# Four small edits in the opening of a two-layer transformer trunk: constant transfers later and in larger pieces, norm weights turned on chip, the shift row turned ahead of the scale row, identity products in TensorE's first wait

## What is computed

```python
for i in range(2):
    mod = silu(c) @ ada_w[i] + ada_b[i]                       # ada_w[i]: 1024 x 6144
    sh_a, sc_a, g_a, sh_f, sc_f, g_f = split(mod, 6)
    h = rmsnorm(x, norm_mix[i]) * (1 + sc_a) + sh_a
    y = diff_attention(h, ...) if i == 0 else retention(h, ..., ret_gn)
    x = x + g_a * y
    h = rmsnorm(x, norm_ffn[i]) * (1 + sc_f) + sh_f
    x = x + g_f * moe(h, router_w[i], ...)                    # 64 experts, 8 per token, one shared
return rmsnorm(x, final_norm)
```

## Time and profile before

| | us |
|---|---|
| median of 3 executions | 1393.24 (1391.47 to 1395.55) |
| the profiled execution | 1395.63 |
| its span in the trace | 1393.7 |
| PE busy in it | 1316.4 |
| DVE, ACT, POOL busy in it | 546.0, 458.4, 227.3 |

### The profile page before, as it was taken

How to read it: one execution, slowest core, us unless ns; L and a number is a source line. 1 busy time by engine, 2 the same in 40 slices (tenths; PEclk the granted TensorE clock), 3 DMA queues, 4 the chain that set the end, 5 groups by cost and what they waited for, 6 DMA issues and landing times.

```text
span 1393.7 us, 32787 instructions
## 1 busy us (share of the span) xinstructions
PE 1316.4 (94%) x11645; PEld 853.6 (61%) x11646; DVE 546.0 (39%) x1259; ACT 458.4 (33%) x938; POOL 227.3 (16%) x684
## 2 busy tenths in 40 slices
PE   4899899999999999899899999999999999999986
PEld 2888675556465555554598778765555565555543
DVE  2565684323232322222634355753323233223324
ACT  3444552222222222212544464622222222222212
POOL 8200103111111211111100000021111111112110
PEclk8899999999999999999999999999999999999998
DMA  9988989999999999999996344599999999999994
GB/s 358 340 316 316 406 363 406 420 421 422 422 422 422 422 422 422 422 422 420 381 377 205 135 151 151 220 402 380 423 422 421 422 421 422 422 423 421 421 422 202
DMA packets 105783, 516.02 MB, mean 370 GB/s; under 512 B 10280, under 2 KB 30880, under 8 KB 55808
## 3 DMA queue, kind: packets, MB, share of 16 engines
q1 hardware_dynamic: 101728, 509.64, 90.8%
q0 software_dynamic: 3296, 3.50, 0.9%
q10 hardware_dynamic: 704, 2.10, 0.4%
HBM read 514.11 MB, written 1.09 MB: 370 GB/s over the span
## 4 chain that ended last, share of the span: by engine, by line
PE 67%; SPq 16%; DMA 9%; DVE 4%; ACT 2%; issue 2%; ACTq 0%; DVEq 0%
PE bank L1007 17%; PE bank L1219 14%; SPq L365 7%; PE bank L1186 7%; PE bank L1145 7%; PE bank L1222 7%; PE bank L1247 6%; SPq L368 4%; DMA ring<-in_exp_w_dram 4%; PE bank L1253 3%; SPq L359 3%; PE bank L981 2%; DMA mods<-in_exp_w_dram 2%; DMA ring<-in_da_w_in_dram 2%; DMA ring<-in_sh_w_dram 1%
## 5 line engine op out<-in xcount | busy, mean ns | idle before, releaser
L1219 PE MATMUL bank<-ring,arena 128*64 128x512 f32 x768 | 184.6, 616 | 15.8 <-DMA ring<-in_exp_w_dram 15.8
L1186 PEld LDWEIGHTS bank<-arena 128*128 128x128 bf16 x3264 | 142.1, 98 | 55.5 <-issue 55.5
L1145 PE MATMUL bank<-arena_r 128*128 128x512 f32 x560 | 159.9, 422 | 3.0 <-DVE arena_r L1683 3.0
L1676 DVE SCALAR_TENSOR_TENSOR arena<-bank,arena 128x128 f32<-128x128 f32 x103 | 32.9, 348 | 327.2 <-ACT arena L762 327.2
L1683 DVE TENSOR_TENSOR arena_r<-bank,arena_r 128x512 fp32r<-128x512 f32 x136 | 94.1, 692 | 154.1 <-ACT arena_r L769 154.1
L1186 PE MATMUL bank<-arena 128*128 128x64 bf16 (+1 forms) x3264 | 151.8, 207 | 0.0
L762 ACT ACTIVATE arena<-bank 128x256 f32<-128x256 f32 (+1 forms) x68 | 22.6, 333 | 387.0 <-PE bank L1219 279.1
L579 POOL TENSOR_TENSOR arena<-arena,pass_base 128x2 f32 x136 | 26.4, 218 | 735.2 <-PE bank L1194 569.0
L769 ACT CAST arena_r<-bank 128x512 fp32r<-128x512 f32 x136 | 79.8, 587 | 175.1 <-PE bank L1247 112.3
L1219 PEld LDWEIGHTS bank<-ring,arena 128*64 128x64 f32 x768 | 66.6, 141 | 113.2 <-issue 107.6
L1663 DVE TENSOR_SCALAR arena<-bank,mod_T 128x128 f32<-128x128 f32 x272 | 92.9, 405 | 70.0 <-PE bank L1186 70.0
(11 more groups left out here) (277 smaller groups left out, 2130.3 us busy)
## 6 DMA issues: line engine op xcount, KB each, us to landing
ring<-in_exp_w_dram SPq DMA_DIRECT2D x264, 1024.0 KB, 24.1
ring<-in_ada_w_dram SPq DMA_DIRECT2D x48, 1024.0 KB, 12.3
mods<-in_exp_w_dram SPq DMA_DIRECT2D x40, 1024.0 KB, 25.0
HH<-in_exp_w_dram SPq DMA_DIRECT2D x40, 1024.0 KB, 21.1
arena<-in_exp_w_dram SPq DMA_DIRECT2D x40, 1024.0 KB, 26.0
ring<-in_ret_w_in_dram SPq DMA_DIRECT2D x24, 1024.0 KB, 12.8
ring<-in_da_w_in_dram SPq DMA_DIRECT2D x12, 1024.0 KB, 14.8
ring<-in_ret_w_out_dram SPq DMA_DIRECT2D x8, 1024.0 KB, 4.9
```

The source lines that it names most:

```text
L1145: ins = nc.tensor.matmul(banks[4 + NH * tc + hf][:, :], S[:, P * tc:P * tc + P], y[:, r, 512 * hf:512 * hf + 512], start=False, stop=(last ...
L1186: ins = nc.tensor.matmul(banks[2 - 2 * half][:, P * kk:P * kk + 2 * W], parts[:, tc, r, P * (4 * half + kk):P * (4 * half + kk + 1)], Pg[: ...
L1219: ins = nc.tensor.matmul(banks[1][W * i:W * i + W, :], xg[:, k, W * i:W * i + W], w13[j][:, k, :, :], start=(k == 0), stop=(k == KD - 1))
```

## The change

1. **Where the constants are transferred.** POOL waits for the end of the first projection (`proj_done` 1) before it starts the vectors for `lam` and the bias rows. `rw`, `rb` and `gn` come behind `store_rows(0, 2, 3, 3)`, which waits for three finished rows. The use of `lvec` on DVE and ACT (`lsum`, `lexp`, `nlam`) moves behind the split of tile 11 and the score masks.
2. **In what pieces.** `rw` is laid out by layer, so a partition's piece is 2 KB. `gn` comes as 16 rows of 512 bytes into the unused `ret_s` and is turned by one PE transpose in layer 1, with a copy on DVE.
3. **Shift row ahead of the scale row.** `turn_h` waits for the identity alone (`ident_ready`). The shift row is turned while the tiles of the scale row land; banks differ. DVE copies block pairs 0 and 1 of `hT`, ACT 2 and 3 (before: DVE 1, ACT 0, 2 and 3).
4. **Identity products.** 52 products of 128x128 (bf16, result unused) behind the turned scale row, ahead of the first projection.

```diff
-        rw = sb("rw", [P, KD, DEPTH * E])
+        rw = sb("rw", [P, DEPTH, KD, E])
+        rw_by_chunk = rw[:, :, :, :].rearrange("p l k e -> p k l e")
...
+        gn_rows = ret_s[0:16, 0:P]
...
+            pool.sem_inc(ident_ready, 1)
...
+            pool.wait_ge(decay_exp, RET_HEADS)
+            for hd in range(RET_HEADS):
+                ins = nc.gpsimd.affine_select(out=decay[:, hd, :], in_=decay[:, hd, :], compare_op=ALU.is_ge, fill=0.0,
+                                              base=0, pattern=[[1, T]], channel_multiplier=-1)
+            ins.then_inc(decay_ready, 1)
+            pool.wait_ge(proj_done, 1)
             for i, v in enumerate((da_lq1, da_lk1, da_lq2, da_lk2)):
                 pool.dma_start(lvec[:, i, :], v.broadcast_to([P, DA_DH])).then_inc(consts_in, 16)
             pool.dma_start(subg[:, :], da_subln.rearrange("a p -> p a"), allow_slow_non_contiguous=True).then_inc(consts_in, 16)
...
-                                              base=0, pattern=[[1, T]], channel_multiplier=-1)
-            ins.then_inc(decay_ready, 1)
+            for q in range(4):
+                pool.dma_start(browB[32 * q:32 * q + 1, :, :],
+                               ada_b[1:2].rearrange("a (s q n) -> q a s n", s=6, q=4)[q]).then_inc(rowsB_in, 16)
+                for i, g in enumerate((norm_mix, norm_ffn)):
+                    pool.dma_start(nrowB[32 * q:32 * q + 1, i, :], g[1:2, 256 * q:256 * (q + 1)]).then_inc(rowsB_in, 16)
+            store_rows(0, 2, 3, 3)
             for l in range(DEPTH):
-                pool.dma_start(rw[:, :, E * l:E * (l + 1)], router_w[l].rearrange("(p k) e -> p k e", k=KD)).then_inc(late_consts_in, 16)
+                pool.dma_start(rw[:, l, :, :], router_w[l].rearrange("(p k) e -> p k e", k=KD)).then_inc(late_consts_in, 16)
                 pool.dma_start(rb[:, l, :], router_b[l:l + 1, :].broadcast_to([P, E])).then_inc(late_consts_in, 16)
-            pool.dma_start(gn[:, :], ret_gn.rearrange("a (c p) -> p (a c)", p=P), allow_slow_non_contiguous=True
-                           ).then_inc(late_consts_in, 16)
-            store_rows(0, 2, 3, 3)
+            pool.dma_start(gn_rows, ret_gn.rearrange("a (c p) -> (a c) p", p=P)).then_inc(late_consts_in, 16)
             store_rows(1, 0, 2, 5)
             store_rows(1, 3, 2, 7)
             pool.wait_ge(rows_stored, 192)
...
-                by_act, by_dve = ((0, 2, 3), (1,)) if n == 0 else ((0, 2), (1, 3))
+                by_act, by_dve = ((2, 3), (0, 1)) if n == 0 else ((0, 2), (1, 3))
 
                 def evict(m):
...
+                        act.wait_ge(hT_dve, 2 * n + by_dve.index(m) + 1)
                     nc.scalar.copy(hT_hi[:, 2 * m:2 * m + 2, :], hT_full[:, 2 * m:2 * m + 2, :]).then_inc(hT_rounded, 1)
 
                 act.wait_ge(mod_T_in[n], 1 if n == 0 else 16)
-                evict(0)
+                evict(by_act[0])
                 round_high(0)
-                evict(2)
...
                 if n == 0:
-                    evict(3)
+                    round_high(1)
+                evict(by_act[1])
+                if n > 0:
+                    round_high(1)
                 round_high(2)
                 round_high(3)
...
-                nc.scalar.copy(rw_hi, rw[:, :, :]).then_inc(rw_rounded, 1)
+                nc.scalar.copy(rw_hi.rearrange("p k (l e) -> p k l e", l=DEPTH), rw_by_chunk).then_inc(rw_rounded, 1)
...
             round_w("mix_in", 0, 1)
-            act.wait_ge(lam_sums, 1)
...
+            nc.scalar.activation(lexp[:, :], lsum[:, :], ACT.Exp).then_inc(lam_exp, 1)
             exps(0)
...
+            act.wait_ge(gn_ready, 1)
...
-            ada(0, 0, banks[4][:, 0:256])
-            pe.wait_ge(pool_consts, 1)
+            ada(0, 0, banks[6][:, 0:256])
+            pe.wait_ge(ident_ready, 1)
             turn_h()
-            ada(0, 1, banks[4][:, 256:512])
-
-            pe.wait_ge(row0_ready, 2)
-            for s in range(2):
+
+            def turn_row0(s):
+                pe.wait_ge(row0_ready, s + 1)
                 for k in range(KD):
                     for q in range(4):
-                        ins = nc.tensor.matmul(banks[5][32 * q:32 * q + 32, KD * s + k:KD * s + k + 1],
+                        ins = nc.tensor.matmul(banks[5 + 2 * s][32 * q:32 * q + 32, k:k + 1],
                                                mrow0[:, s, k:256:KD], ident[:, 32 * q:32 * q + 1], start=True, stop=True)
-            ins.then_inc(rows0_turned, 1)
+                ins.then_inc(rows0_turned, 1)
+
+            turn_row0(0)
+            ada(0, 1, banks[4][:, 0:256])
+            pe.wait_ge(pool_consts, 1)
+            turn_row0(1)
+            for _ in range(52):
+                nc.tensor.matmul(banks[6][:, 0:P], ident16[:, :], ident16[:, :], start=True, stop=True)
 
...
+            pe.wait_ge(late_consts_in, 16 * 5)
+            nc.tensor.transpose(banks[7][:, 0:16], gn_rows, ident[0:16, 0:16]).then_inc(gn_turned, 1)
...
+                    evict(0)
                 evict(1)
                 if n == 0:
...
+            nc.vector.tensor_tensor(mrow0[:, 0, :], banks[6][:, 0:256], brow0[:, 0, :], ALU.add).then_inc(row0_ready, 1)
+            dve.wait_ge(rows0_turned, 1)
+            nc.vector.tensor_copy(mod_T[:, 0, 0, :], banks[5][:, 0:KD])
             dve.wait_ge(ada_done, 2)
-            step(nc.vector.tensor_tensor(mrow0[:, 1, :], banks[4][:, 256:512], brow0[:, 1, :], ALU.add))
+            step(nc.vector.tensor_tensor(mrow0[:, 1, :], banks[4][:, 0:256], brow0[:, 1, :], ALU.add))
             nc.vector.scalar_tensor_tensor(out=mrow0[:, 1, :], in0=mrow0[:, 1, :], scalar=1.0, in1=nrow0[:, 0, :],
                                            op0=ALU.add, op1=ALU.mult).then_inc(row0_ready, 1)
-            nc.vector.tensor_tensor(mrow0[:, 0, :], banks[4][:, 0:256], brow0[:, 0, :], ALU.add).then_inc(row0_ready, 1)
-            dve.wait_ge(rows0_turned, 1)
-            nc.vector.tensor_copy(mod_T[:, 0, 0:2, :], banks[5][:, 0:2 * KD].rearrange("p (s k) -> p s k", s=2)
-                                  ).then_inc(mod_T_in[0], 1)
+            dve.wait_ge(rows0_turned, 2)
+            nc.vector.tensor_copy(mod_T[:, 0, 1, :], banks[7][:, 0:KD]).then_inc(mod_T_in[0], 1)
             evict_hT()
 
...
-            dve.wait_ge(consts_in, 16 * 5)
-            step(nc.vector.tensor_tensor(lprod, lvec[:, 0:4:2, :], lvec[:, 1:4:2, :], ALU.mult))
-            nc.vector.tensor_reduce(lsum[:, :], lprod, AX_X, ALU.add).then_inc(lam_sums, 1)
-            nc.vector.tensor_scalar(subs[:, :], subg[:, :], 1.0 - LAM_INIT, None, ALU.mult)
-
-            dve.wait_ge(lam_exp, 1)
-            step(nc.vector.tensor_tensor(nlam[:, :], lexp[:, 1:2], lexp[:, 0:1], ALU.subtract))
-            step(nc.vector.tensor_scalar(nlam[:, :], nlam[:, :], -LAM_INIT, None, ALU.add))
 
             def finish_a(n):
...
             mask_scores(0)
             mask_scores(1)
+            dve.wait_ge(lam_exp, 1)
+            step(nc.vector.tensor_tensor(nlam[:, :], lexp[:, 1:2], lexp[:, 0:1], ALU.subtract))
+            step(nc.vector.tensor_scalar(nlam[:, :], nlam[:, :], -LAM_INIT, None, ALU.add))
             for part in range(3):
                 n, i = 4 * part, 3 * part + 4
                 finish_a(n)
...
+            dve.wait_ge(gn_turned, 1)
+            nc.vector.tensor_copy(gn[:, :], banks[7][:, 0:16]).then_inc(gn_ready, 1)
```

More of the change, by code:

```diff
@@ L240, in trunk @@
         row2_1_in, row5_1_in = sem("row2_1_in"), sem("row5_1_in")
-        pool_consts, pool_step = sem("pool_consts"), sem("pool_step")
+        pool_consts, pool_step, ident_ready = sem("pool_consts"), sem("pool_step"), sem("ident_ready")
+        gn_turned, gn_ready = sem("gn_turned"), sem("gn_ready")
         rows_zero = sem("rows_zero")
@@ L515, in _ @@
                                allow_small_or_imprecise_dtypes=True).then_inc(decay_arg, 1)
-            for q in range(4):
-                pool.dma_start(browB[32 * q:32 * q + 1, :, :],
-                               ada_b[1:2].rearrange("a (s q n) -> q a s n", s=6, q=4)[q]).then_inc(rowsB_in, 16)
-                for i, g in enumerate((norm_mix, norm_ffn)):
-                    pool.dma_start(nrowB[32 * q:32 * q + 1, i, :], g[1:2, 256 * q:256 * (q + 1)]).then_inc(rowsB_in, 16)
+            pool.wait_ge(decay_exp, RET_HEADS)
[4 more added lines that the diff above has]
+            pool.wait_ge(proj_done, 1)
             for i, v in enumerate((da_lq1, da_lk1, da_lq2, da_lk2)):
@@ L789, in _ @@
             round_w("mix_in", 0, 1)
-            act.wait_ge(lam_sums, 1)
-            nc.scalar.activation(lexp[:, :], lsum[:, :], ACT.Exp).then_inc(lam_exp, 1)
             def evict_proj0(i):
@@ L1527, in evict_hT @@
                 dve.wait_ge(mod_T_in[n], 1 if n == 0 else 16)
+                if n == 0:
+                    evict(0)
                 evict(1)
@@ L1547, in split_rw @@
                 dve.wait_ge(rw_rounded, l + 1)
-                nc.vector.tensor_tensor(rw_lo, rw[:, :, :], rw_hi, ALU.subtract).then_inc(rw_split, 1)
```

(9 more changed lines are left out.)

9 lines of the change are left out of this document (3 added, 6 removed).

## The result

The changed kernel takes 1412.80 us (median of 4 executions, 1411.72 to 1413.58) where the kernel before takes 1393.11: a ratio of 1.0145, 95% interval 1.0129 to 1.0161. The prediction was 1390.1, range 1386.3 to 1393.8. The profiled execution took 1412.48 us, its span 1410.8: 17.1 us more than the span before, where the medians differ by 19.7, mostly because the profiled execution of before was 2.5 us above its kernel's median.

What follows compares the result with a forecast made beforehand. The stream was taken to bound the expert loops, PE layer 1's mixer, and a chain of waits the opening. Terms 3.6 - 1.5 - 0.1 + 1.1 = 3.1 us off the median 1393.24 gave 1390.1 us, range 1386.3 to 1393.8.

Steps and rivals of the forecast that it cites:

- The step that failed: Whole kernel: the opening's gain is carried on if stream and PE start the expert loop earlier; after that only one transpose changes.
- D: Opening: constants land late and DVE stands at `consts_in`; `turn_a(1)` 9.7 us late, 1404.5 us; chance 0.07.
- The first product: First projection: its first product starts at 35.8 us in place of 37.09, a gain of 1.3 us.
- The clock of the first projection: First projection: identity products raise the clock from 0.50 to full, 2.95 us less PE work; projection ends 3.8 us earlier.
- The rate from 44 to 51 us: Stream ahead of tile 16: above 350 GB/s in place of 271, with the `lam` vectors moved there.
- The masks and `turn_a(1)`: Opening: DVE's masks start at 53.8 us, `turn_a(1)` at 63.6 in place of 67.19, a gain of 3.6 us.
- The second half-speed stretch: PE from 66.90 to 73.80 us: half clock loses 3.4 us, of which 1.1 us is taken as gained.
- rival B: Ahead of `turn_a(1)`: idle time shrinks, second half-speed stretch is gone; gain 5.4 us, to 1387.8 us; chance 0.37.
- The stream from 125 us: Saturated stream ahead of `sh_w`: 0.60 MB more to carry, so 1.5 us are paid back.
- what the pieces add: Saturated stream ahead of `sh_w`: cost of the moved transfers' pieces beyond their bytes, taken as 0 from 0 to 2.3 us.
- Rival C: Saturated stream: the moved transfers cost the same 3.8 us in the later place; 1393.5 us; chance 0.14.
- The opening by itself: Whole kernel: opening's gains less what the stream pays back and one transpose, a gain of 3.1 us.

## Why the prediction was wrong

**The step that failed** is the sentence that what the opening gains is carried on, since from there on nothing in the change touches anything but one transpose. The identity products were costed by the time they take, and as covered by PE's wait. Their 104 instructions push every later instruction of PE along, the two loops too, and no rival had that in it. Putting those instructions in without any other part of the change, as products or as idle waits, gives 20 and 17 us; taking the products out gives them back. The chance of 0.06 for slower stood for another mechanism, D, which didn't happen: DVE waited 0.56 us for `subg`, which landed 8.56 us behind the start of its issue.

**The first product.** Predicted 35.8, measured 37.20. The scale row's last products took 1.94 us from 27.90 at half speed, where I had 1.07, and ended 1.7 us later than worked out: 0.9 by the clock and 0.8 because their tile landed at 27.9 and not at 27.1 (the stream ran at 357 GB/s from 26 to 28 us, and I had taken 407). Before it was 37.09, so nothing was gained at this place.

**The clock of the first projection.** As predicted: 48 products took 6.00 us, and the granted clock was 0.81 from 35 to 38 us and 1.00 soon after.

**The rate from 44 to 51 us.** Predicted above 350 GB/s, measured 303, with the `lam` vectors and the bias rows in it. ACT's split of tile 16 waited for no transfer all the same.

**The masks and `turn_a(1)`.** DVE's masks were due at 53.8 and came at 54.84; `turn_a(1)` was due at 63.6 and came at 64.50, 2.7 us earlier than before where I had 3.6.

**The second half-speed stretch.** I took a third of 3.4 us. It was gone: the clock is 1.00 from 66.9 to 73.8 us and the 64 ada products take 3.59 us, with 1.50 us of idle PE ahead of `turn_a(1)` in place of 2.28. That is rival B's mechanism. But the kernel before with 208 waits has a clock of 1.00 there as well, from 64 to 75 us, with nothing added but the waits at PE's start, so part of the 3.4 us may be the draw of one execution.

**The stream from 125 us.** The mis-sized term is what the pieces add. I took 0 from a range of 0 to 2.3; it was 1.4 (1.0 to 1.4 in three traces), and it went when `rb` and `gn`, whose share I had put at 0.3 or nothing, were moved. With the bytes, 3 us are paid back in place of 1.5. Rival C had this, at 3.8.

**The opening by itself.** With the loops back in 7 blocks the change is worth 0.9998 (0.9983 to 1.0013), where the forecast was a gain of 3.1 us, just beyond that interval. In its profile it is 2.6 us ahead at the last update of X in the mixer and level at the end of layer 0's experts (681.55 against 681.19), and the two profiled executions are 2.0 and 2.5 us above their medians. By the summed rates the stream is still 0.9 MB, some 2 us, ahead at 640 us, so the lead goes behind that; what takes it wasn't found.

**A reading.** The prediction counts four of the first six slices at 316 to 363 GB/s; in the earlier trace rows it is five. No sum rests on it.

## What to carry to other kernels

An instruction has a place as well as a duration. Where an engine's loop body comes near to the size of its instruction memory, count the instructions ahead of the loop and the blocks that the body touches before and after every edit, however idle the engine is where the edit stands; idle time "issue" at the loop's first instruction and a growing count on the instruction queue show it at once. Small transfers belong where the stream will later stand still anyway, not where it is last: moving five of them out of such a stretch took this kernel from level to 0.25% faster. In one profile a lead of 2 or 3 us can be the draw of that execution.

## What was not expected of the hardware

- PE's loop body of 1,634 instructions runs without a fetch when it touches 7 blocks of 256 instructions; when it touches 8, some 9 packets of 16 KB are fetched per round and PE stands 5.6 to 6.6 us at most branches back and 1.5 to 3.3 us once more soon after, 31 to 36 us a layer in all. With layer 1's loop at 240 of 256, near the next block, it was 10.4 to 10.9 us in one piece, 42.2 in all; why stays open.
- Over the 15 or 16 us that begin with such a stall the granted clock is 0.61 to 0.68.
- Two waits of PE for a satisfied semaphore made one instruction, and 104 such instructions at the start of PE's program, where it is idle, kept it from its first products for 6.2 us and let the shift row end when it had before.
- With `rb` and `gn`, 72 KB together, behind `rw`, a stream of 408 GB/s fell to 235 for 3 us and lost some 1.4 us, where the bytes of the two are worth 0.2; with `rw` alone (one trace) it didn't.
